# The last four units of the last output group, in halves of 128 tokens, with the final norm per half

## What is computed

```python
    y = jnp.concatenate([y_a * jax.nn.silu(z_a), y_r * jax.nn.silu(z_r)], axis=-1)
    out = jnp.einsum('bsf,fd->bsd', y, w_out)
    return x + gate[:, None] * out
...
    return rms_norm_2(h, final_gain)
...
def rms_norm_2(x, g):
    xf = x.astype(jnp.float32)
    y = xf * lax.rsqrt(jnp.mean(xf * xf, axis=-1, keepdims=True) + NORM_EPS)
    return (y * g.astype(jnp.float32)).astype(x.dtype)
```

## Time and profile before

| what | before |
|---|---|
| median of 3 runs | 1539.68 us (1539.65 to 1540.36) |
| the profiled execution | 1539.14 us |
| its span | 1537.3 us |
| TensorE matmul busy | 1524.7 us (99%) |
| VectorE / ScalarE / GpSimd busy | 1136.3 (74%) / 779.0 (51%) / 29.8 us (2%) |
| DMA | 339.23 MB, mean 221 GB/s |
| chain that ended last, by line | L1334 6%, L1338 6%, L1336 6%, L1380 2%, L1382 2%, L1383 2% |

### The profile page before, as it was taken

How to read it: one execution, slowest core, us unless ns; L and a number is a source line. 1 busy time by engine, 2 the same in 40 slices (tenths; PEclk the granted TensorE clock), 3 DMA queues, 4 the chain that set the end, 5 groups by cost and what they waited for, 6 DMA issues and landing times. The chain is left out here.

```text
span 1537.3 us, 32072 instructions
## 1 busy us (share of the span) xinstructions
PE 1524.7 (99%) x12586; PEld 1485.4 (97%) x12586; DVE 1136.3 (74%) x1373; ACT 779.0 (51%) x930; POOL 29.8 (2%) x56
## 2 busy tenths in 40 slices
PE   9999999999999999999999999999999999999997
PEld 8999997999999999999999999999999989999997
DVE  7877777657987878888788878879864644765754
ACT  7645455545554444444444444445554643454554
POOL 0000000000000000000000000000000000000000
PEclk9999999999999999999999999999999999999999
DMA  9474556457777767677686776866465554445451
GB/s 350 168 271 160 202 173 224 140 170 280 299 278 248 285 239 273 237 259 272 229 294 229 268 272 222 300 219 218 151 246 193 193 193 164 163 157 187 156 186 58
DMA packets 85932, 339.23 MB, mean 221 GB/s; under 512 B 9680, under 2 KB 10208, under 8 KB 79328
## 3 DMA queue, kind: packets, MB, share of 16 engines
q1 hardware_dynamic: 77760, 281.05, 51.2%
q0 software_dynamic: 7232, 54.55, 9.9%
q10 hardware_dynamic: 864, 2.53, 0.4%
HBM read 335.97 MB, written 2.12 MB: 220 GB/s over the span
## 5 line engine op out<-in xcount | busy, mean ns | idle before, releaser
L693 DVE TENSOR_TENSOR wlo<-raw,whi 128x1024 fp32r<-128x1024 f32 x528 | 643.3, 1223 | 346.8 <-ACT whi L329 343.2
L329 ACT ACTIVATE whi<-raw 128x1024 fp32r<-128x1024 f32 x528 | 558.3, 1061 | 646.8 <-PE PS L1338 574.7
L1334 PE MATMUL PS<-gh,whi 128*128 128x256 f32 x3096 | 864.1, 279 | 1.0 <-DVE wlo L693 0.8
L1336 PE MATMUL PS<-gl,whi 128*128 128x256 f32 x3096 | 856.8, 277 | 0.0
L1338 PE MATMUL PS<-gh,wlo 128*128 128x256 f32 x3096 | 856.7, 277 | 0.0
L1334 PEld LDWEIGHTS PS<-gh,whi 128*128 128x128 f32 x3096 | 582.2, 188 | 5.8 <-issue 2.6
L1336 PEld LDWEIGHTS PS<-gl,whi 128*128 128x128 f32 x3096 | 581.8, 188 | 0.8
L1338 PEld LDWEIGHTS PS<-gh,wlo 128*128 128x128 f32 x3096 | 581.4, 188 | 0.0
L1334 PE MATMUL PS<-ah,whi 128*128 128x256 f32 x688 | 189.9, 276 | 0.0
L1338 PE MATMUL PS<-ah,wlo 128*128 128x256 f32 x688 | 189.9, 276 | 0.0
L1336 PE MATMUL PS<-al,whi 128*128 128x256 f32 x688 | 189.9, 276 | 0.0
(11 more groups left out here) (256 smaller groups left out, 895.6 us busy)
## 6 DMA issues: line engine op xcount, KB each, us to landing
raw<-weights SPq DMA_DIRECT2D x528, 512.0 KB, 3.8
ada_w<-w_ada POOLq DMA_DIRECT2D x48, 1024.0 KB, 6.2
EM<-rows POOLq DMA_DIRECT2D x1, 3072.0 KB, 12.3
X<-xT SPq DMA_DIRECT2D x3, 512.0 KB, 8.2
c<-const ACTq DMA_DIRECT2D x1, 1536.0 KB, 7.2
c_act<-c_rows POOLq DMA_DIRECT2D x1, 1024.0 KB, 6.4
outT<-X SPq DMA_DIRECT2D x2, 512.0 KB, 3.2
outT<-X SPq DMA_DIRECT2D x3, 256.0 KB, 2.2
```

What stands on the lines that cost most here:

```text
L329: act.activation(whi[:, j % SPLIT, first:first + 1024], raw[:, j, :], ACT.Copy).then_inc(s_hi, 1)
L693: dve.tensor_tensor(wlo[:, j % SPLIT, first:first + 1024], raw[:, j, :], whi[:, j % SPLIT, first:first + 1024].bitcast(F32), ALU.subtract) ...
L1334: pe.matmul(out[:, t, :], whi[:, b, w], hi[:, kt, :], start=first and half == 0 and (apart or t % 2 == 0), stop=False, skip_group_check=True)
L1336: pe.matmul(out[:, t, :], whi[:, b, w], lo[:, kt, :], start=False, stop=False, skip_group_check=True)
```

## The change

Units 28 to 31 of group 3 leave `product` and `last_pair`. `last_half(0)` runs all four for tokens 0 to 127, in banks 0 to 3, which group 2 has left; `last_half(1)` runs them for tokens 128 to 255 tile by tile, in `own`, behind what units 24 to 27 have summed there. What those units have summed for tokens 0 to 127 VectorE adds to X first (`half_early`). The final norm is done for each half: its column sum (`half_sum(0)`) and its turn (`half_turn(0)`) stand inside the second half's matmuls, behind (tile 1, unit 1) and (tile 2, unit 1). Squares, gains, root, reciprocal, copy and scaling exist once per half, GpSimd's step too, and the output leaves in nine pieces of 128 tokens.

```diff
-FINAL = ((4, 1), (5, 1), (6, 2), (8, 2), (10, 2))
+FINAL = (((4, 4), (8, 4), (12, 3)), ((4, 2), (6, 3), (9, 3), (12, 3)))
...
-            for n, (first, tiles) in enumerate(FINAL):
-                sp.wait_ge(s_fin, n + 1)
-                sp.dma_start(outT[:, first:first + tiles, :], X[:, first:first + tiles, :]).then_inc(s_out, 16)
-            sp.wait_ge(s_pool, 1)
-            sp.dma_start(outT[:, 0:4, :], X[:, 0:4, :]).then_inc(s_out, 16)
-            sp.wait_ge(s_fin, len(FINAL) + 2)
-            sp.dma_start(outT[:, 12:16, :], X[:, 12:16, :]).then_inc(s_out, 16)
-            sp.wait_ge(s_out, 16 * (len(FINAL) + 2))
+            for c in range(2):
+                m, done = slice(P * c, P * c + P), c * (len(FINAL[0]) + 1)
+                for n, (first, tiles) in enumerate(FINAL[c][:-1]):
+                    sp.wait_ge(s_fin, done + n + 1)
+                    sp.dma_start(outT[:, first:first + tiles, m], X[:, first:first + tiles, m]).then_inc(s_out, 16)
+                    if n == len(FINAL[c]) - 2:
+                        sp.wait_ge(s_pool, c + 1)
+                        sp.dma_start(outT[:, 0:4, m], X[:, 0:4, m]).then_inc(s_out, 16)
+                sp.wait_ge(s_fin, done + len(FINAL[c]) + 1)
+                sp.dma_start(outT[:, 12:16, m], X[:, 12:16, m]).then_inc(s_out, 16)
+            sp.wait_ge(s_out, 16 * (len(FINAL[0]) + len(FINAL[1]) + 2))
...
-            pool.wait_ge(s_copy, 1)
-            x = X[:, 0:4, :]
-            pool.tensor_tensor(x, x, rb[:, :].unsqueeze(1).to_broadcast([P, 4, S]), ALU.mult).then_inc(s_pool, 1)
+            for c in range(2):
+                pool.wait_ge(s_copy, c + 1)
+                x = X[:, 0:4, P * c:P * c + P]
+                pool.tensor_tensor(x, x, rb[:, P * c:P * c + P].unsqueeze(1).to_broadcast([P, 4, P]), ALU.mult
+                                   ).then_inc(s_pool, 1)
...
+            def half_square(c, t):
+
+                m = slice(P * c, P * c + P)
+                act.wait_ge(s_tile, 4 + 4 * c + t + 1)
+                act.activation(near_tile(3, t)[:, m], X[:, 12 + t, m], ACT.Square).then_inc(s_sq, 1)
+                if t < 3:
+                    gained(12 + t, SQUARES[3] + 3 + 4 * c + t + 1, m)
+
+            def half_root(c):
+
+                act.wait_ge(s_ss, 4 + c)
+                act.activation(rcol[:, 1, c:c + 1], PS[:, 0, c:c + 1], ACT.Sqrt, bias=col("eps"),
+                               scale=1.0 / D).then_inc(s_rcol, 1)
+
+            def half_copy(c):
+
+                act.wait_ge(s_spread, 3 + 2 * c)
+                act.activation(rb[:, P * c:P * c + P], PS[:, 2, P * c:P * c + P], ACT.Copy).then_inc(s_copy, 1)
...
-            column_root(3)
-            act.wait_ge(s_spread, 3)
-            act.activation(rb[:, :], own[:, 0, :], ACT.Copy).then_inc(s_copy, 1)
+            for t in range(4):
+                half_square(0, t)
+            half_square(1, 0)
+            half_root(0)
+            half_square(1, 1)
+            half_copy(0)
+            half_square(1, 2)
+            half_square(1, 3)
+            half_root(1)
+            half_copy(1)
...
+            def half_early():
+
+                dve.wait_ge(s_used, 8 * B_OUT2 + 28 + SPLIT)
+                for t in range(4):
+                    k = 12 + t
+                    dve.scalar_tensor_tensor(X[:, k, 0:P], own[:, t, 0:P], modT[:, 32 + k:33 + k], X[:, k, 0:P], ALU.mult,
+                                             ALU.add).then_inc(s_part, 1)
+
+            def half_tile(c, t):
+
+                m, k = slice(P * c, P * c + P), 12 + t
+                if c == 0:
+                    dve.wait_ge(s_part, 13 + t)
+                dve.wait_ge(s_own, 3 + 4 * c + t + 1)
+                dve.scalar_tensor_tensor(X[:, k, m], own[:, t, m] if c else PS[:, t, m], modT[:, 32 + k:33 + k], X[:, k, m], ALU.mult, ALU.add
+                                         ).then_inc(s_tile, 1)
+
+            def half_near(c, t):
+
+                m = slice(P * c, P * c + P)
+                dve.wait_ge(s_sq, SQUARES[3] + 3 + 4 * c + t + 1)
+                dve.wait_ge(s_near, 2 + 4 * c + t)
+                dve.tensor_tensor(SQX4[:, 0, 0, m], SQX4[:, 0, 0, m], near_tile(3, t)[:, m], ALU.add).then_inc(s_near, 1)
+
+            def half_inverse(c):
+
+                dve.wait_ge(s_rcol, 2 + c)
+                dve.reciprocal(rcol[:, 1, c:c + 1], rcol[:, 1, c:c + 1]).then_inc(s_icol, 1)
+
+            def half_scaled(c, n):
+
+                m = slice(P * c, P * c + P)
+                if n < len(FINAL[c]):
+                    first, tiles = FINAL[c][n]
+                    dve.wait_ge(s_gain, 12 if first < 12 else 15 + 3 * c)
+                    x = X[:, first:first + tiles, m]
+                    dve.tensor_tensor(x, x, half_spread(c).unsqueeze(1).to_broadcast([P, tiles, P]), ALU.mult
+                                      ).then_inc(s_fin, 1)
+                    return
+                dve.wait_ge(s_sq, SQUARES[3] + 3 + 4 * c + 4)
+                dve.scalar_tensor_tensor(X[:, 15, m], X[:, 15, m], col("final", 15), half_spread(c), ALU.mult, ALU.mult
+                                         ).then_inc(s_fin, 1)
+
+            fold(3, 2, SQX4)
+            half_early()
+            dve.wait_ge(s_fold, 4)
+            for t in range(4):
+                half_tile(0, t)
+                if t:
+                    half_near(0, t - 1)
+            half_near(0, 3)
+            half_tile(1, 0)
+            half_inverse(0)
+            half_tile(1, 1)
+            half_near(1, 0)
+            half_tile(1, 2)
+            dve.wait_ge(s_spread, 2)
+            half_scaled(0, 0)
+            half_near(1, 1)
+            half_tile(1, 3)
+            for n in range(1, len(FINAL[0]) + 1):
+                half_scaled(0, n)
+            half_inverse(1)
+            dve.wait_ge(s_spread, 4)
+            for n in range(len(FINAL[1]) + 1):
+                half_scaled(1, n)
...
+            def last_half(c):
+
+                m = slice(P * c, P * c + P)
+                unit = 8 * B_OUT2 + 28
+                if c == 0:
+                    pe.wait_ge(s_evac, G_OUT2 + 2 + 3)
+                    for u in range(4):
+                        pe.wait_ge(s_lo, unit + u + 1)
+                        if u < 3:
+                            for half in range(2):
+                                for t in range(4):
+                                    half_product(c, t, u, half)
+                            continue
+                        for t in range(4):
+                            for half in range(2):
+                                mm = half_product(c, t, u, half)
+                            mm.then_inc(s_own, 1)
+                    return
+                pe.wait_ge(s_part, 16)
+                for t in range(4):
+                    for u in range(4):
+                        for half in range(2):
+                            mm = half_product(c, t, u, half)
+                        if (t, u) == (1, 1):
+                            half_sum(0)
+                        if (t, u) == (2, 1):
+                            half_turn(0)
+                    mm.then_inc(s_own, 1)
+                half_sum(1)
+                half_turn(1)
+
+            def half_product(c, t, u, half):
+
+                m, kt = slice(P * c, P * c + P), 8 + 2 * u + half
+                w = slice(512 * half + P * t, 512 * half + P * t + P)
+                out = own[:, t, m] if c else PS[:, t, m]
+                pe.matmul(out, whi[:, u, w], gh[:, kt, m], start=(c == 0 and u == 0 and half == 0), stop=False,
+                          skip_group_check=True)
+                pe.matmul(out, whi[:, u, w], gl[:, kt, m], start=False, stop=False, skip_group_check=True)
+                return pe.matmul(out, wlo[:, u, w], gh[:, kt, m], start=False, stop=(u == 3 and half == 1),
+                                 skip_group_check=True)
+
+            def half_sum(c):
+
+                m = slice(P * c, P * c + P)
+                pe.wait_ge(s_near, 8 if c else 6)
+                if c:
+                    pe.wait_ge(s_rcol, 2)
+                order = (None, 2, 3) if c else (None,)
+                for n, t in enumerate(order):
+                    if t is not None:
+                        pe.wait_ge(s_sq, SQUARES[3] + 3 + 4 * c + t + 1)
+                    src = SQX4[:, 0, 0, m] if t is None else near_tile(3, t)[:, m]
+                    mm = pe.matmul(PS[:, 0, c:c + 1], src, ones[:, 0:1], start=(n == 0),
+                                   stop=(n == len(order) - 1), skip_group_check=True)
+                mm.then_inc(s_ss, 1)
+
+            def half_turn(c):
+
+                pe.wait_ge(s_icol, 2 + c)
+                for out in (half_spread(c), PS[:, 2, P * c:P * c + P]):
+                    pe.matmul(out, rcol[:, 1, c:c + 1].to_broadcast([P, P]), ident, start=True, stop=True
+                              ).then_inc(s_spread, 1)
...
-            for s in range(30):
+            for s in range(28):
```

(60 more changed lines are left out.)

20 lines of the change are left out of this document (5 added, 15 removed).

## The result

The changed kernel takes 1548.33 us (median of 4 runs, 1547.49 to 1548.71) against 1539.66 for the kernel before (4 runs, 1538.44 to 1540.36): ratio 1.0057, interval 1.0045 to 1.0069, slower by 8.7 us. The forecast was 1549.5 in a range of 1543.5 to 1554. Now and then an execution of any of these programs, the kernel before too, takes 1.7% longer; the medians in this document leave such executions out, and the one profile that fell into one (e1_cut_128) is not read.

What follows compares the result with a forecast made beforehand. TensorE's stream of weight units was taken to bound the kernel (99% of the span). Last product at 1537.4 plus a 9.7 us tail gave a span of 1547.1 and a time of 1549.5 us, range 1543.5 to 1554.

Steps and rivals of the forecast that it cites:

- Term 1: Last group's products: 96 become 192 of 128 tokens, each paying its own weight load of 0.111 us.
- columns-only rival: Half products: loads stay hidden, only columns count, 0.057 us each; 1539.2 us, no difference; chance 7%.
- float32 rate: Rival on half products: 128-column float32r runs as slowly as float32, 0.222 us each; 1570.8 us; chance 7%.
- middle spacing: Half products 0.084 us apart, between columns' 0.057 and loads' 0.111; 1544.2 us; given with the 5% sustained-figure rival.
- 81 ns: Rival on half products: loads overlap more deeply in a long stream, 0.081 us each; 1543.6 us; chance 5%.
- Term 2: First half's column sum and two turns among the second half's products: 6 records, 0.67 us, no wait.
- T: Start of the projection's last product: 1526.29 before, forecast 1537.4, 11.1 us later.
- Term 3: VectorE in the tail: first half done at T + 2.3, second half scaled by T + 5.3, against T + 7.0 before.
- Term 4: Output DMAs in the tail: 512-byte packets at 30 ns, last bytes T + 8.9, end T + 9.7 against 11.0 before.
- The sum: End of span 1537.4 + 9.7 = 1547.1, profiled execution 1548.9, plus 0.54 to the median: 1549.5 us.

Runs made afterwards that it cites:

- e1_cut_128: Kernel before with products of units 28 to 31 cut into two of 128 tokens, by mistake also in the first layer's output projection: 1560.42 us, ratio 1.0136.
- e1b: Kernel before with only the last group's 96 products cut into two of 128 tokens, norm and output as before: 1550.35 us, ratio 1.0071.
- e2: Kernel before with products of units 28 to 31 cut into 192 and 64 tokens, first layer's output projection included: 1560.63 us, ratio 1.0140.
- e5: Changed kernel with only units 30 and 31 in halves, units 28 and 29 whole as before: 1543.36 us, ratio 1.0025 to the kernel before.
- a2_changed_again: The changed kernel run a second time, nothing altered: 1548.44 us, ratio 1.0058 to the kernel before.
- e3: Kernel before with the output in five pieces, each sent as two DMAs of 128 tokens (512-byte rows): 1542.01 us, ratio 1.0014.
- e3b: Kernel before with the output in five pieces of whole rows of 256 tokens: 1540.47 us, ratio 1.0004.
- e7: Changed kernel with output sent only as the second half's scalings end, in five pieces of whole rows: 1549.09 us, ratio 1.0066 to the kernel before.

## Why the prediction was right

**Term 1, the loads** (0.111 us each, bounds 0.105 and 0.125): right, 0.111 in the trace ((1537.30 - 1515.35) / 197), and e1, e1b, e2 and e5 show it as the price per product. The columns-only rival (0.057), the float32 rate (0.222) and the middle spacing (0.084) are all excluded. The 81 ns that the Trainium skill gives in "TensorE: Matmul & The Clock Gate" ("Back-to-back issue gap") for a stream at N=128 is not reached by these float32r products: 111 ns in both halves, and as much in e1b over 192 products without a break (21.28 us for 191 steps).

**Term 2, sum and turn inside the products** (0.67 us, no wait): right; T was 1537.30 for 1537.4, with no idle time of TensorE. That the place agrees to 0.1 us is luck: it was 1537.73 in a2_changed_again.

**Term 3, VectorE's side**: the end was right (T + 5.0 for T + 5.3), two steps on the way were not. VectorE was through with the first half at T + 1.9 and not T + 2.3, and the turn's matmuls took 0.81 us where I had put 0.36. The two cancelled, and scaling began at 1540.24, T + 2.9. That none of it lies on the path shows in the second execution: in a2_changed_again the turns took 0.50 us, and its last bytes stood at T + 8.75 all the same. The two turns from the chain of either, at a granted clock of 0.50 in the first and 1.00 in the second:

```profile
1539.41 0.81 PE PS L1550 x2
```
```profile
1539.84 0.50 PE PS L1550 x2
```

**Term 4, the DMAs' side**: right in kind, high in size: 28.8 ns for 30, last bytes at T + 8.7 for T + 8.9, end at T + 9.5 for T + 9.7. The rule of the Trainium skill's page "DMA: Bandwidth & Descriptors" ("Specifications"), line rate from 512 B on, would make it 24.5; the trace disagrees, the short rows cost more, 7.3 us of work for the output against 5.5 before. One thing was left out and did no harm by luck: GpSimd was called "not last" at T + 4.8 (T + 5.0 measured), but its drain behind that ends at T + 9.2, 0.03 us ahead of SyncE's. Had the packets cost the 24.5 ns of the lower bound, GpSimd's drain would have held the end where it is.

**The sum**: span 1546.8 for 1547.1. The median came out 1.2 us below the forecast: 0.3 is the span's, 0.2 the step from span to execution (1.66 for 1.84), and 0.7 comes from the 0.54 us that I had added for the distance between profiled execution and median, which did not come again (1548.46 and 1548.33).

## What to carry over

A stationary load has a price of its own, and a product that moves fewer columns than it takes to hide the load costs the same as a full one; before work is split along the moving side, read the load's spacing where nothing covers it (loads of one-column matmuls) and count the extra loads on the bounding engine. Splitting to overlap a tail must gain more than those loads: here 3.8 us came back for 12.7. And before a tail is shortened, find everything that ends with it: here the DMAs and GpSimd's drain ended together, so a gain of 1.0 us on the DMAs alone was worth 0.5 to 0.65. Short rows are part of the price too (1.5 us between e3 and e3b); a version that starts the output earlier and keeps its rows whole was not run.

## What the runs showed of the hardware that I had not expected

*TensorE's clock falls at different moments behind the same program.* Behind the last product, the granted clock stayed at 1.00 (2.4 GHz) until 1531.4, 5.1 us after T, in the profiled run of before, but was at half (1.2 GHz) by T + 2.5 in e3b, whose products are the same, and by T + 1.2 in e1b. The windows view over the norm's turns in before, e3b and e1b:

```profile
1528.70:1529.50 0.80, 0.75 (x6) 0.75 (x7) 0.00 (x1) 0.00 (x0) 0.00 (x0) 1.00 0.00 0
```
```profile
1528.30:1529.60 1.30, 1.25 (x6) 1.25 (x7) 0.00 (x0) 0.00 (x0) 0.00 (x0) 0.52 0.00 0
```
```profile
1539.20:1540.50 1.30, 1.28 (x6) 1.29 (x7) 0.02 (x1) 0.00 (x0) 0.00 (x0) 0.50 0.00 0
```

The four turns took 0.72 us at the full clock and 1.24 at half. Up to T + 2.5 TensorE did the same in before and e3b, so it is not the width of the products; what else decides it stays open. It makes 0.5 us of a run's tail a matter of luck. It isn't only the tail: between 1095 and 1105 us, far ahead of the change, the granted clock averages 0.83 in the profiled execution of the changed kernel and in e3b's, 1.00 in those of before and e3, and VectorE's remainders number 381 to 401, which span that time, lie 62.3 and 62.2 us apart against 61.7. That is part of T's wandering.

*The time that SyncE needs to issue a piece is not fixed.* The issue of 12 to 15 took 0.66 us in the changed kernel (1542.97 above) and 0.35 before, for half the bytes. Pieces of short rows took 0.37 to 0.87 us in these traces, whole ones mostly 0.33 to 0.45, but one whole piece, the last of e7, 0.93, so the rows are not all of it. In the changed kernel the issues don't set the end, since the DMA engines have no gap behind them.
